# A two-block transformer kernel: the first layer's mixer with its projection units in another order and its local attention between them

## The reference

```python
def even_mixer(u, w_in, w_out, lb, onorm_g, sinks, cos_b, sin_b):
    qa, fa, ia, ga, qb, kb, vb = jnp.split(u @ w_in, EVEN_SPLITS, axis=-1)
    oa = hgrn2_chunkwise(qa, fa, ia, lb)          # q = silu(qa), f = lb + (1-lb)*sigmoid(fa)
    oa = rmsnorm_2(oa, onorm_g) * silu(ga)
    ob = swa_with_sinks(apply_rope(qb), apply_rope(kb), vb, sinks)
    return jnp.concatenate([oa, ob], axis=-1) @ w_out
```

## Time and profile before

| | |
|---|---|
| median of 3 runs | 1922.31 us |
| the profiled execution, its time | 1922.47 us |
| the profiled execution, its span | 1920.4 us |
| mean granted TensorE clock | 0.966 of full |
| PE busy | 1807.7 us, 94% |
| VectorE busy | 946.0 us, 49% |
| ScalarE busy | 727.2 us, 38% |
| read and written in HBM | 223 GB/s over the span |

### The profile page before, as it was taken

The page is one execution under the profiler, slowest core; times in us unless marked ns, Lnnn a source line. Parts: engine busy times, 40 slices in busy tenths (PEclk is TensorE's granted clock), DMA queues, the critical chain, the costliest instruction groups (busy, mean ns, idle before and its releaser), DMA issues.

```text
span 1920.4 us, 25424 instructions
## 1 busy us (share of the span) xinstructions
PE 1807.7 (94%) x10198; PEld 1389.2 (72%) x10198; DVE 946.0 (49%) x1185; ACT 727.2 (38%) x943; POOL 42.2 (2%) x55
## 2 busy tenths in 40 slices
PE   8957799999999999999968999989999999999997
PEld 8845544544544468888947888878888999888886
DVE  5474211111111167566565665766656564575665
ACT  4442111111111154345443443564435445453444
POOL 2000000000000000000000000000000000300000
PEclk9978799999999999999959999999999999999999
DMA  8523689999999965555503555535555544545561
GB/s 274 159 88 136 280 345 422 422 422 422 422 422 421 422 204 186 194 179 166 176 23 104 173 179 195 191 124 190 188 184 169 185 156 152 176 170 189 183 197 55
DMA packets 191809, 429.41 MB, mean 224 GB/s; under 512 B 7796, under 2 KB 146132, under 8 KB 167168
## 3 DMA queue, kind: packets, MB, share of 16 engines
q1 hardware_dynamic: 187952, 418.41, 59.8%
q0 software_dynamic: 3792, 10.08, 1.9%
HBM read 426.62 MB, written 1.84 MB: 223 GB/s over the span
## 4 chain that ended last, share of the span: by engine, by line
PE 80%; DMA 7%; DVE 7%; ACT 4%; issue 1%; SPq 0%; DVEq 0%; POOL 0%; ACTq 0%
PE pw L487 57%; PE acc L487 22%; DMA mring<-in_w_eu 7%; DVE wl L1555 1%; ACT arena L1295 1%; PE pw L777 1%; DVE x L1977 0%; DMA raw<-in_w_in 0%; ACT sm L1287 0%; ACT wh L1110 0%; ACT arena L1362 0%; DVE scr L1989 0%; ACT L1140 0%; DVE scr L2045 0%; ACT arena L1381 0%
## 5 line engine op out<-in xcount | busy, mean ns | idle before, releaser
L487 PE MATMUL pw<-aa,wh 128*128 128x512 f32 (+1 forms) x2512 | 701.1, 349 | 8.2 <-DVE aa L1583 7.4
L487 PE MATMUL pw<-aa,wl 128*128 128x256 f32 x1960 | 552.2, 282 | 0.0
L1555 DVE TENSOR_TENSOR wl<-raw,wh 128x2048 fp32r<-128x2048 f32 x205 | 463.5, 2298 | 169.3 <-ACT wh L1110 168.0
L487 PEld LDWEIGHTS pw<-aa,wh 128*128 128x128 f32 x2512 | 438.6, 190 | 75.2 <-DVE wl L1555 7.9
L1110 ACT ACTIVATE wh<-raw 128x2048 fp32r<-128x2048 f32 x205 | 381.1, 1905 | 35.3 <-DMA raw<-in_w_in 17.7
L487 PEld LDWEIGHTS pw<-aa,wl 128*128 128x128 f32 x1960 | 372.8, 190 | 1.5
L487 PE MATMUL acc<-wh,aa 128*128 128x512 f32 x1088 | 350.4, 396 | 12.5 <-DVE aa L1581 4.0
L487 PE MATMUL pw<-mring,arena 128*64 128x512 f32 x1536 | 338.3, 595 | 6.6 <-DMA mring<-in_w_eu 5.9
L487 PEld LDWEIGHTS pw<-mring,arena 128*64 128x64 f32 x1536 | 108.5, 137 | 209.7 <-issue 206.2
L487 PEld LDWEIGHTS acc<-wh,aa 128*128 128x128 f32 x1088 | 206.4, 190 | 60.5 <-DVE aa L1581 4.5
L487 PE MATMUL acc<-wl,aa 128*128 128x512 f32 x544 | 213.8, 393 | 0.0
(11 more groups left out here) (388 smaller groups left out, 1306.8 us busy)
## 6 DMA issues: line engine op xcount, KB each, us to landing
raw<-in_ffn_w_in SPq DMA_DIRECT2D x88, 1024.0 KB, 5.1
mring<-in_w_eg SPq DMA_DIRECT2D x64, 1024.0 KB, 16.2
mring<-in_w_eu SPq DMA_DIRECT2D x64, 1024.0 KB, 18.1
mring<-in_w_ed SPq DMA_DIRECT2D x64, 1024.0 KB, 16.9
raw<-in_ffn_w_out SPq DMA_DIRECT2D x44, 1024.0 KB, 4.9
raw<-in_odd_w_in SPq DMA_DIRECT2D x24, 1024.0 KB, 5.3
raw<-in_w_in SPq DMA_DIRECT2D x12, 1024.0 KB, 12.9
raw<-in_even_w_in SPq DMA_DIRECT2D x11, 1024.0 KB, 5.4
```

Source lines behind the costliest of these rows:

```text
L487: return pe.matmul(out, lhs, rhs, start=start, stop=stop, skip_group_check=True)
L1555: dve.tensor_tensor(wl[:, u % RING, :], raw[:, u % RING, :], wh[:, u % RING, :].bitcast(F32), ALU.subtract).then_inc(sig(f"{ep}_lo"), 1)
```

## The change

The units of the first layer's mixer are taken in the order 8, 9, 10, 2, 3, 0, 1, 4, 5, 6, 7. SP's queue loads them so, and position p in that order takes the place of the unit's number in the ring and in the banks. The units now use two banks of `pw`, p mod 2; the logits use the other two, and the attention's products go to banks 2 and 3 of `acc`. TensorE waits for the evacuation of position p-2 before position p, where it was four places before.

The rotation stands behind position 3. The logits of heads 0 and 1 stand behind position 5, those of the later pairs behind positions 6, 7 and 8. The transposes and products of a pair stand behind the logits of the next one, behind positions 6 to 9; both heads are transposed first, then both are multiplied. ScalarE's and VectorE's programs are written in the order that goes with it. The recurrence's query is evacuated as a plain copy, and its Silu is made later, as one operation in ScalarE's program behind the last pair's exponentials. The attention's output takes chunks 8 to 11, and the last output unit's split on VectorE stands behind the recurrence's masks.

```diff

         block = ctx.enter_context(nc.Block())

...
                 for j in range(UB[(l, "mix_out")] - UB[(l, "mix_in")]):
-                    load("b", UB[(l, "mix_in")] + j, cols_unit(w1, j * 256))
+                    load("b", UB[(l, "mix_in")] + j, cols_unit(w1, (j if l else EVEN_ORDER[j]) * 256))
...
-                for j in range(11):
-                    if j >= 4:
-                        w.more("proj_evac")
+                seen = [0]
+
+                def evacuated(n):
+                    if n > seen[0]:
+                        w.more("proj_evac", n - seen[0])
+                        seen[0] = n
+
...
+                def logits(s):
+
+                    if s == 0:
+                        w.more("roped")
+                    else:
+                        w.more("pairs_used", 2)
+                    for h in (2 * s, 2 * s + 1):
+                        rows_ = slice(64 * (h % 2), 64 * (h % 2) + 64)
+                        q, k, g = qr[rows_, (h // 2) * T:(h // 2 + 1) * T], kr[rows_, :], h // 4
+                        b = pw[:, 2 + h % 2, :]
+                        mm(b[:, 0:P], q[:, 0:P], k[:, g * T:g * T + P])
+                        mm(b[:, P:P + T], q[:, P:T], k[:, g * T:(g + 1) * T]).then_inc(sig("pairs_ready"), 1)
+
...
+                def values(s):
+
+                    for h in (2 * s, 2 * s + 1):
+                        w.more("weights_ready")
+                        for j in range(3):
+                            last = pe.transpose(acc[:, h % 2, j * P:(j + 1) * P], swl[h % 2][:, j * P:(j + 1) * P], ident)
+                        last.then_inc(sig("weights_turned_psum"), 1)
+                    for h in (2 * s, 2 * s + 1):
+                        w.more("weights_turned")
...
+                        out = acc[64 * (h % 2):64 * (h % 2) + 64, 2 + c // 2, (c % 2) * T:(c % 2 + 1) * T]
...
+                        mm(out[:, 0:P], vb[:, 0, g * 64:g * 64 + 64], pT[:, 0:P])
+                        mm(out[:, P:T], vb[:, 0, g * 64:g * 64 + 64], pT[:, P:T], True, False)
+                        last = mm(out[:, P:T], vb[:, 1, g * 64:g * 64 + 64], pT[:, T:T + P], False, True)
+                        if h % 4 == 3:
+                            last.then_inc(sig("sw_out"), 1)
+
+                for p in range(11):
+                    j = EVEN_ORDER[p]
+                    if p >= 2:
+                        evacuated(p - 1)
                     if j in (4, 5):
-                        last = tokens("b", u0 + j, j % 4)
+                        last = tokens("b", u0 + p, p % 2)
                     elif j < 10:
-                        last = features("b", u0 + j, j % 4, arriving=j == 0)
...
                     else:
-                        features("b", u0 + j, j % 4, 0, 1)
-                        last = tokens("b", u0 + j, j % 4, P, P, T)
+                        features("b", u0 + p, p % 2, 0, 1)
+                        last = tokens("b", u0 + p, p % 2, P, P, T)
                     last.then_inc(sig("b_used"), 1)
-                w.more("proj_evac", 4)
...
+                    if p == 3:
+                        rotated()
+                    if 5 <= p < 9:
+                        logits(p - 5)
+                    if 6 <= p < 10:
+                        values(p - 6)

                 w.more("hgrn_ready")
+                w.more("pairs_used", 2)
...
-                    b = pw[:, h % 2, :]
+                    b = pw[:, 2 + h % 2, :]
...
-                w.more("act_ready", 2)
+                evacuated(11)
...
-                rows("b", o0, 4, True, False)
-                rows("b", o0 + 1, 6, False, False)
+                rows("b", o0, 8, True, False)
+                rows("b", o0 + 1, 10, False, False)
...
-                def evac(j):
-                    used("b", u0 + j)
-                    src = pw[:, j % 4, :]
+                def evac(p):
+                    used("b", u0 + p)
+                    j = EVEN_ORDER[p]
+                    src = pw[:, p % 2, :]
...
-                        func = {0: ACT.Silu, 1: ACT.Sigmoid, 3: ACT.Silu, 4: ACT.Copy}[j // 2]
+                        func = {0: ACT.Copy, 1: ACT.Sigmoid, 3: ACT.Silu, 4: ACT.Copy}[j // 2]
...
-                for j in range(3, 11):
-                    split("b", u0 + j)
-                    evac(j - 3)
-                    if j == 7:
...
+                o0 = UB[(0, "mix_out")]
+                for p in range(3, 11):
+                    split("b", u0 + p)
+                    evac(p - 3)
+                    if p == 7:
                         w.more("dve_result")
                         act.activation(kd, fk, ACT.Ln).then_inc(sig("act_result"), 1)
-                    if j == 8:
-
+                    if p == 8:
+                        exponentials(0)
+                    if p == 9:
+                        weights_copied(0)
                         w.more("dve_result")
                         b16 = bsum.rearrange("p (g c) -> p g c", c=64)
                         act.activation(eb, bsum, ACT.Exp).then_inc(sig("act_result"), 1)
@@ -1443,30 +1480,28 @@
                         act.activation(sm[:, 136:152].unsqueeze(2), b16[:, :, 63:64], ACT.Exp).then_inc(sig("act_result"), 1)
...
-                for j in range(8, 11):
-                    evac(j)
-                for j in range(4):
-                    split("b", UB[(0, "mix_out")] + j)
-
-                for h in range(8):
-                    k = 96 + 8 * (h % 2)
-                    w.more("exponents_ready")
-                    for t, (c0, n) in enumerate(((0, P), (P, T))):
...
+                        exponentials(1)
+                    if p == 10:
+                        weights_copied(1)
+                        exponentials(2)
+                split("b", o0)
+                evac(8)
+                weights_copied(2)
+                exponentials(3)
+                act.activation(qs, qs, ACT.Silu).then_inc(sig("act_result"), 1)
+                split("b", o0 + 1)
+                evac(9)
+                weights_copied(3)
                 w.more("sw_out", 2)
                 for b in range(2):
-                    act.activation(ah[:, 4 + 2 * b:6 + 2 * b, :], two(pw[:, 2 + b, :]), ACT.Copy).then_inc(sig("high"), 1)
+                    act.activation(ah[:, 8 + 2 * b:10 + 2 * b, :], two(acc[:, 2 + b, :]), ACT.Copy).then_inc(sig("high"), 1)
+                split("b", o0 + 2)
+                evac(10)
+                split("b", o0 + 3)
...
-                    w.more("act_result", 4)
+                    w.more("act_result", 5)
...
-                for j in range(3, 11):
-                    split("b", u0 + j)
-                    if j == 6:
-
-                        w.more("proj_evac", 4)
...
-                    if j == 7:
-                        log_sums()
-                    if j == 9:
-                        decayed()
-                w.more("proj_evac", 7)
-                w.more("psum_for_dve")
...
+                def forget():
+
+                    w.more("proj_evac", 5)
+                    for h in range(NH):
+                        f = fk[:, h * T:(h + 1) * T]
+                        dve.tensor_scalar(f, f, sm[:, 128 + h:129 + h], sm[:, 124 + h:125 + h], ALU.mult, ALU.add).then_inc(sig("dve_step"), 1)
+                    w.more("dve_step", 4)
...
+                o0 = UB[(0, "mix_out")]
+                for p in range(3, 7):
+                    split("b", u0 + p)
+                roped()
+                split("b", u0 + 7)
+                forget()
                 soft(0)
-                for h in range(8):
-                    if h + 1 < 8:
-                        soft(h + 1)
-                    k = 96 + 8 * (h % 2)
-                    w.more("exponentials", 3)
-                    then(dve.tensor_tensor(sm[:, k + 2:k + 4], sm[:, k + 2:k + 4], sm[:, k + 4:k + 6], ALU.add))
-                    then(dve.reciprocal(sm[:, k + 6:k + 8], sm[:, k + 2:k + 4]))
-                    for t, (c0, n) in enumerate(((0, P), (P, T))):
-                        e = swl[h % 2][:, c0:c0 + n]
-                        dve.tensor_scalar(e, e, sm[:, k + 6 + t:k + 7 + t], None, ALU.mult).then_inc(sig("dve_step"), 1)
-                    w.more("dve_step", 2)
-                    dve.sem_inc(sig("weights_ready"), 1)
-                    if h < 4:
-                        split("b", UB[(0, "mix_out")] + h)
-                w.more("weights_turned_psum", 2)
+                split("b", u0 + 8)
+                weighed(0)
+                log_sums()
+                soft(1)
+                split("b", u0 + 9)
+                weighed(1)
+                soft(2)
+                split("b", u0 + 10)
+                weighed(2)
+                soft(3)
+                split("b", o0)
+                weighed(3)
+                decayed()
+                split("b", o0 + 1)
                 w.more("high", 2)
                 for b in range(2):
-                    dve.tensor_tensor(al[:, 4 + 2 * b:6 + 2 * b, :], two(pw[:, 2 + b, :]),
```

(46 more changed lines are left out.)

112 lines of the change are left out of this document (45 added, 67 removed).

## The result

The changed kernel took 1893.66 us, the median of 4 executions (1891.31 to 1897.64), beside 1922.83 for the kernel before on the same chip: a ratio of 0.9843 [0.9827, 0.9858], 29 us or 1.6% less. The forecast was 1897.5, in a range of 1893.5 to 1904. A later series of the same kernel, five executions on one chip, had a median of 1897.91 (1892.62 to 1899.63) beside 1924.51 before: 0.9858 [0.9836, 0.9879]. The forecast's own ratio, 1897.5 over 1922.3, is 0.9871: outside the first interval, inside the second. The median lies just above the range's near end in us, but measured by the ratio, against the before of its own series, it lies just beyond it: 1893.5 over 1922.31 is 0.9850. The profiled execution took 1894.32, with a span of 1892.2 against 1920.4.

The account below looks back on a forecast made before the run. PE was taken as the bound, with waits and half clock in the mixer. The walk saves 27.6 us, one clock lapse costs 2.5, leaving 25.1: 1922.5 - 25 = 1897.5 us, range 1893.5 to 1904.

Parts of the forecast that it names:

- The walk (Part 2): PE's mixer, slot by slot: output rows start at 991.4, 97.1 us after the first unit against 124.7, 27.6 less.
- Part 1: Two unit banks instead of four: PE waits 1.3 us ahead of the third unit, for the first evacuation.
- Part 3: PE's clock: one lapse to 0.50 at the second pair costs 2.5 us, bounds 0 to 10, leaving 25.1 saved.
- Part 4: ScalarE's table loads and VectorE's moved split: fewer loads save nothing, the split is hidden, no extra drain of 1.38 us.
- The first (no lapse, 1895.5): Rival: PE's clock never lapses in the mixer; gain 27.6 less some 0.6 for handovers, 1895.5 us; chance 0.22.
- The second: Rival: clock lapses in three or four slots, or slot handovers cost twice as much; about 1903 us; chance 0.15.
- The third (VectorE late everywhere): Rival: VectorE becomes the bound, every slot late by 3 us; 3 x 2.4 more lost, 1905 us; chance 0.05.
- The fourth: Rival: once down, the clock stays at 1.2 GHz from the first pair on; slower by 18, 1941 us; chance 0.02.
- The fifth: Rival: no effect, the time is given back at the output rows by weights landing or split late; chance 0.02.

Follow-up runs that it names:

- e3: Changed kernel with three needless VectorE operations ahead of the second pair's maxima; 1892.77 us once, stretch 99.17.
- e8: Changed kernel with the edits of e5, e6 and e7 together; 1892.19 us, median of 4, ratio 0.9852, stretch 93.59.
- e12: Changed kernel with six needless VectorE operations ahead of the second pair's maxima; 1899.0 us once, stretch 102.01.
- e9: Changed kernel again without an edit, a later series of five executions; median 1897.91 us, ratio 0.9858.
- e10: Changed kernel once more without an edit; 1892.7 us once.
- e6: Changed kernel with the first evacuation ahead of ScalarE's trigonometry; 1894.88 us once.
- e7: Changed kernel with the fourth pair's copies on ScalarE ahead of the split of an output unit; 1898.94 us once.
- e4: Changed kernel with the third pair's logits computed four times, filling the second slot's wait with half-row matmuls; 1895.27 us once.
- e5: Changed kernel with the decay sums' sixteen scans on VectorE moved ahead of the first pair's maxima; 1893.57 us once.
- e11: The kernel of e5 again; 1891.21 us, median of 5, ratio 0.9828.
- e1: Kernel before, in its old order, with matmuls of zeros in PE's waits to keep the clock up; 1922.93 us against 1924.9, ratio 0.9987.

## Why the prediction came out as it did

The profiles of the interleaved kernels but for e3, e8 and e12. "Load" is VectorE's wait for a small load ahead of the trigonometry. "Slot" is from the second pair's turn, its row of logits ahead of the transposes, to the third's; the lapse is what it has over 12.28, and none where the clock stayed at 1.00.

| run | stretch | load | wait ahead of third unit | slot | lapse |
|---|---|---|---|---|---|
| changed kernel, first | 96.20 | 2.26 | 0.44 | 12.28 | 0 |
| e9, again | 98.05 | 2.58 | 0.76 | 13.80 | 1.52 |
| e10, again | 97.35 | 2.40 | 0.58 | 13.27 | 0.99 |
| e6 | 97.96 | 2.31 | none | 14.74 | 2.46 |
| e7 | 98.20 | 2.22 | 0.39 | 14.32 | 2.04 |
| e4, wait filled | 96.70 | 2.77 | 0.94 | 12.28 | 0 |
| e5 / e11, wait gone | 94.25 / 94.83 | 2.23 / 2.79 | 0.40 / 0.98 | 9.21 / 9.22 | 0 |

- **The walk (Part 2) was right in sum, partly by luck.** Take the third-unit wait and the lapse out of the three profiles of the changed kernel, and 95.76, 95.77 and 95.78 are left; the prediction has 97.1 - 1.3 = 95.8. Piece by piece: the second slot's waits are 2.38 and 0.55 (forecast 2.6 and 0.5), the fourth's 1.05 (0.9), the third's 0.25 (none); the first slot's transposes and products take 944.13 to 946.73 (944.2 to 946.8); HGRN starts at 982.88 (982.9) and takes 8.45 to the rows (8.5). But the sum is closer than its parts: the seven units from the fifth on took 1.0 more in all than I gave them (5.84 to 5.95 each beside a slot, not 5.76), the rotation 0.4 and the slots 0.5 less (a pair's products 1.25 to 1.52, not 1.6). The waits that I name also add up to 5.9, not to the sum's 5.5: of the first slot's 0.6 the walk has only 0.1, and that slot took 2.60, as the walk has it.
- **Part 1, a mis-sized term.** I had 1.3 us of waiting ahead of the third unit; it was 0.44, 0.76 and 0.58, 0.7 less in the mean. From the first unit's start to that evacuation's end I had 13.0, one execution's number; from start to third unit it was 12.1 to 12.7 in the profiles with this order. It moves with a small load. ScalarE's trigonometry ahead of the evacuation hangs on VectorE, whose first operation there waits for that load, before and in the changed kernel:

```profile
899.49 0.30 DVE L2094 CAST arena<-arena 128x256 f32<-128x256 int32 x1 [2.96 <-DMA sm<-in_attn_sinks]
```

```profile
899.60 0.29 DVE L2129 CAST arena<-arena 128x256 f32<-128x256 int32 x1 [2.26 <-DMA sm<-in_attn_sinks]
```

In every row of the table but e6's the wait ahead of the third unit is the load's less 1.8. The 2.96 that my 13.0 holds is the longest of all 14 profiles; e1, in the old order, has 2.22.
- **Part 3, the failed term: one lapse, 2.5 us.** The place was right and the size was possible, but it is no fixed cost. Of the five profiles with this second slot (first, e9, e10, e6, e7) four show it, at 0.99 to 2.46; the mean over the five is 1.4, over the three of the unedited kernel 0.84. I took nearly the upper bound of one event, 1.7 plus up to 1, as if it came whole and each time. The first profile was one without it.
- Together: 0.7 and 1.7 (2.5 less 0.84) make the mean stretch of the changed kernel, 97.2, 2.4 shorter than the 99.6 forecast. That is a gain of 27.4 instead of 25.1. The other 1.4 of the 3.8 us between 1897.5 and the first median isn't in this stretch; scatter outside it is larger than that (the mixer starts from 890.7 to 898.2, and from the rows on it is 899.5 to 904.3), and the second median lies 0.4 above the forecast. How near a median comes to 1897.5 says little, then.
- **Part 4 was right.** Table load and split cost PE nothing beyond the fourth slot's wait of 1.05, for which Part 2 had 0.9; the split's share of that is 0.64 (e7). The drain of 1.38 of the Trainium skill (ScalarE: Activation LUTs, What ACT_TABLE_LOAD costs) doesn't show: by it that wait would be 1.4 longer and the saving 23.7, and the Silu's row stands at the load's end.
- **Rivals.** The first (no lapse, 1895.5) describes the first profile, and e9 and e10 are of the forecast's kind, at a lower price: they are two outcomes of one program, not two theories. The second is refuted: no profile shows a lapse in another slot. The rule of the Trainium skill (TensorE: Matmul & The Clock Gate, Part 4) that transposes don't count would have made all four slots likelier to lapse; the first, third and fourth have six transposes each beside little idling, and none lost the clock. No run had transposes alone, so the rule itself isn't refuted. The third (VectorE late everywhere) holds for the second slot only, and e3 and e12 show what it would have cost. The fourth is refuted: the clock came back every time, within the ninth unit. The fifth is refuted by the span.
- **What the lapse goes with**: of seven profiles whose second slot has a bare wait of about 2.4 us or more, six lapsed (e3 and e12 among them); with the wait filled (e4) or gone (e5, e11, e8) none of four did. A fall came behind a wait of 1.26 beside thin work in e1, and none with one of 3.09 ahead of dense rows in e6. Why one execution keeps its clock where the same rows lose it in the next stays open, and so does the scatter outside the mixer.

## What to carry to other kernels

A stage that ran at half the clock and waited on VectorE is first a question of overlap: holding the clock up in place gave 2.5 us of the 28.4; laying the stage between dense units gave 16.6, and the clock came with it. Walk the bottleneck engine's program with durations from the trace, slot by slot: it held here to 0.1 us in sum, with parts up to 1 us off that cancelled. Price an event that may or may not happen by its chance times its size, with both outcomes in the range's body, and profile the same kernel more than once before its absence is taken for a cause.

## What was not expected of the hardware

- The granted clock is not a function of the program: with the same instructions and the same waits of 2.4 and 0.55 us it stayed at 1.00 once and fell to 0.50 twice, for about 3.5 us; in e6 and e7 for almost 7. After the same wait of 3.09 ahead of the next stage it stayed up in one of 14 profiles, was down for about 3.5 us in ten and for over 6 in three.
- At full clock, too, two heads' logits on the two halves of the rows cost one's: the pair took 0.93 (x8), one head in e1 0.92 (x4).
- With half-row matmuls, 3.00 us of them, in place of the bare wait the clock stayed at 1.00 in the one profile of e4; with the bare wait it did so in one of five.
